# Loading the input beside the first mixer's prologue, and the last norm inside the MLP, in a four-layer decoder trunk

## What is computed

```python
def reference(x, ...):                     # x: (8, 2048, 1024) float32
    for i in range(4):
        h = rmsnorm(x, norm_mix[i])
        y = (mixer_a, mixer_b, mixer_c)[i % 3](h, ...)   # A in layers 0 and 3
        x = x + y
        h = rmsnorm(x, norm_mlp[i])
        x = x + jnp.square(jax.nn.relu(h @ m_w1[i])) @ m_w2[i]
    return rmsnorm(x, norm_final)

def rmsnorm(x, g):
    return x * lax.rsqrt(jnp.mean(x * x, axis=-1, keepdims=True) + EPS) * g

def mixer_a(h, w_in, b_in, vn_g, vn_b, w_s, b_s, w_out):
    u, v = jnp.split(jax.nn.gelu(h @ w_in + b_in), 2, axis=-1)   # 3072 each
    v = layernorm(v, vn_g, vn_b)
    w = jnp.where(causal, w_s, 0)          # 8 groups of 128 x 128
    gate = einsum over each chunk of 128 tokens of w and v, plus b_s
    return (u * gate) @ w_out
```

## Time and profile before

| | |
|---|---|
| runs shown | 4108.21 and 4675.72 us, median 4391.97 us |
| the profiled execution, its own time | 4105.52 us |
| its span on the slowest core (6) | 4104.0 us |
| spans of the eight cores | 4067.6 to 4104.0 us |
| mean granted TensorE clock, cores | 0.932 to 0.943 of 2.4 GHz |
| busy share of core 6 | TensorE 91%, DVE 55%, ACT 25%, POOL 6% |

### The profile page before, as it was taken

The page is one execution under the profiler, slowest core; times in us unless marked ns, Lnnn a source line. Parts: engine busy times, 40 slices in busy tenths (PEclk is TensorE's granted clock), DMA queues, the critical chain, the costliest instruction groups (busy, mean ns, idle before and its releaser), DMA issues.

```text
span 4104.0 us, 48667 instructions; the slowest of 8 cores (4067.6 to 4104.0 us)
## 1 busy us (share of the span) xinstructions
PE 3716.4 (91%) x16824; PEld 1640.3 (40%) x16824; DVE 2253.4 (55%) x2975; ACT 1037.3 (25%) x1543; POOL 242.5 (6%) x278
## 2 busy tenths in 40 slices
PE   5899998999976799998998969999789999899995
PEld 3334443444432244443333324444334444344443
DVE  3425524756566765655556566566354353565655
ACT  2433332211111121112223231111243333211113
POOL 0011111000000000000000000000001111000000
PEclk7899998999988799999999979999789999899997
DMA  7689989122226512223323322220769899612202
GB/s 151 94 119 127 144 119 128 21 42 42 35 44 91 77 21 42 42 32 59 46 40 49 48 38 42 37 36 1 108 90 130 111 137 131 90 32 42 35 8 82
DMA packets 302184, 283.38 MB, mean 69 GB/s; under 512 B 4854, under 2 KB 281462, under 8 KB 301944
## 3 DMA queue, kind: packets, MB, share of 16 engines
q0 software_dynamic: 295104, 262.16, 44.5%
q1 hardware_dynamic: 6844, 18.12, 1.3%
HBM read 534.02 MB, written 8.39 MB: 132 GB/s over the span
## 4 chain that ended last, share of the span: by engine, by line
PE 84%; DVE 9%; ACT 3%; issue 3%; DMA 1%; ACTq 0%; DVEq 0%; SPq 0%; POOL 0%; POOLq 0%
PE bank L83 84%; DVE rsd L83 2%; ACT rsq L83 2%; DVE m_hT L83 1%; DVE hTp L83 1%; DVE c_dg L83 1%; DMA xin<-x 1%; DVE f_h L83 1%; DVE b_tA L83 1%; ACT c_yb L83 0%; DVE c_rstd L83 0%; DVE b_pooled L83 0%; DVE b_tB L83 0%; ACT rsd L83 0%; DVE b_y L83 0%
## 5 line engine op out<-in xcount | busy, mean ns | idle before, releaser
L83 DVE TENSOR_TENSOR xT<-bank,xT 128x512 f32<-128x512 f32 x1152 | 794.3, 691 | 462.7 <-PE bank L83 458.2
L83 PE MATMUL bank<-m_aT,ring 128*128 128x512 bf16 x4096 | 910.2, 381 | 15.2 <-DVE m_rl L83 15.2
L83 PE MATMUL bank<-m_hT,ring 128*128 128x512 bf16 x4096 | 908.3, 380 | 0.0
L83 PE MATMUL bank<-hTp,ring 128*128 128x512 bf16 x2560 | 624.4, 398 | 70.5 <-DVE hTp L83 39.5
L83 ACT ACTIVATE m_aT<-m_rl 128x512 bf16<-128x512 f32 x512 | 321.8, 629 | 1420.3 <-DVE m_rl L83 1420.3
L83 DVE TENSOR_SCALAR m_rl<-bank 128x512 f32<-128x512 f32 x512 | 352.5, 691 | 518.8 <-PE bank L83 394.9
L83 PEld LDWEIGHTS bank<-m_aT,ring 128*128 128x128 bf16 x4096 | 401.8, 98 | 504.0 <-issue 25.0
L83 PEld LDWEIGHTS bank<-m_hT,ring 128*128 128x128 bf16 x4096 | 401.9, 98 | 486.1 <-issue 5.6
L83 PEld LDWEIGHTS bank<-hTp,ring 128*128 128x128 bf16 x2560 | 252.6, 102 | 360.3 <-issue 152.5
L83 PE MATMUL bank<-ring,hTp 128*128 128x512 bf16 x1536 | 369.3, 384 | 19.8 <-DVE hTp L83 19.8
L83 PE MATMUL bank<-a_uT,ring 128*128 128x512 bf16 x1536 | 347.8, 391 | 9.2 <-DVE a_uT L83 9.2
(11 more groups left out here) (89 smaller groups left out, 1813.5 us busy)
## 6 DMA issues: line engine op xcount, KB each, us to landing
ring<-a_w_in POOLq DMA_DIRECT2D x96, 1024.0 KB, 11.2
ring<-m_w POOLq DMA_DIRECT2D x64, 1024.0 KB, 9.2
ring<-a_w_out POOLq DMA_DIRECT2D x64, 768.0 KB, 7.7
ring<-c_w_in POOLq DMA_DIRECT2D x16, 1024.0 KB, 10.8
xin<-x SPq DMA_DIRECT2D x16, 512.0 KB, 5.7
ring<-b_w_in POOLq DMA_DIRECT2D x8, 1024.0 KB, 8.7
ring<-b_w_out POOLq DMA_DIRECT2D x8, 1024.0 KB, 9.3
ring<-c_w_out POOLq DMA_DIRECT2D x8, 1024.0 KB, 10.0
```

Source lines behind the costliest of these rows:

```text
L83: return lambda e: getattr(e, _method)(*args, **kwargs)
```

## The change

1. **Input and first prologue together.** In layer 0 `mixer_a` calls the input phase itself. The prologue is now a generator with three yields. Its first part (four loads, the memsets) is issued after x chunk 1, the part to the masked matrices after chunk 6, the column sums after chunk 10, a_S after chunk 13; the norm of tile 0 after chunk 3.
2. **The mask.** The affine select on POOL becomes a multiplication on DVE, straight from PSUM, by a mask tile that POOL makes once at the start.
3. **Layer 3.** The norm of tile 0 stands ahead of the whole prologue, which has the new mask too.
4. **The last norm.** The output phase is a function `tail(tt)`, called in the last layer's MLP right after W2 of fb 7 for that tile. It transposes the raw xT, takes the sum of squares on ACT from PSUM (one number per token), the root and reciprocal on 128 x 1, and scales on DVE from PSUM by that number and by a tile that holds the norm's weights in every partition, loaded once.

```diff
     for c in range(NCH):
         ...
+        if after_chunk is not None:
+            after_chunk(c)
...
+            def rn0():
+                rmsnorm(rb_persist, 0, gcol, lambda kc: hTp[0][:, kc, :], lambda kc: hTp_res[0][kc])
...
+                def prologue():
...
+                    sc.op("sp", I("dma_start", out=wst[:], in_=dram["a_w_s"][ia].rearrange("g t s -> t g s")),
+                          wr=[wst_res], dma=asem)
+                    sc.op("sp", I("dma_start", out=bsrc[:], in_=dram["a_b_in"][ia:ia + 1, AW:2 * AW]),
+                          wr=[bsrc_res], dma=asem_b)
+                    sc.op("dve", I("memset", sel1[:], 1.0), wr=[sel1_res])
+                    sc.op("dve", I("memset", rrow[:], 0.0), wr=[rrow_res])
+                    sc.op("dve", I("memset", lrow[:], 0.0), wr=[lrow_res])
+                    sc.op("dve", I("memset", lrow[32:33, :], 1.0), wr=[lrow_res])
+                    sc.op("sp", I("dma_start", out=rrow[32:33, :], in_=dram["a_b_s"][ia:ia + 1, :]), wr=[rrow_res], dma=asem_r)
+                    sc.op("sp", I("dma_start", out=lrow[0:1, :], in_=dram["a_vn_b"][ia:ia + 1, :]), wr=[lrow_res], dma=asem_l)
+                    yield
+                    sc.op("dve", I("tensor_copy", out=brow[:], in_=bsrc[:]), rd=[bsrc_res], wr=[brow_res])
...
-                sc.op("pool", I("affine_select", out=wmf2[:], in_=wmf[:], pattern=[[0, 8], [1, 128]],
-                                                        compare_op=ALU.is_ge, fill=0.0, base=0, channel_multiplier=-1),
-                      rd=[wmf_res], wr=[wmf2_res])
+                        sc.op("dve", I("tensor_tensor",
+                            out=wmf2[:, half * 4:half * 4 + 4, :], in0=bk[:].rearrange("p (a b) -> p a b", a=4),
+                            in1=cmask[:].unsqueeze(1).broadcast_to([128, 4, 128]), op=ALU.mult),
+                            rd=[bres, const_res], wr=[wmf2_res])
...
+                gen = prologue()
+                if with_input:
+                    def after_chunk(c):
+                        if c in (1, 6, 10, 13):
+                            next(gen, None)
+                        if c == 3:
+                            rn0()
+                    input_phase(pro, after_chunk)
...
+                else:
+                    rn0()
+                    for _ in gen:
+                        pass
...
-            RN(0)
             V(0)
...
+                if tail is not None and fb == 7:
+                    tail(tt)
...
+                if final:
+                    for half in range(2):
+                        bk, bres = bks[half]
+                        sc.op("act", I("activation", out=junk[half][:], in_=bk[:], func=AF.Square,
+                                       accum_out=ss[:, ob, half:half + 1]),
+                              rd=[bres], wr=[junk_res[half], ss_res[ob]])
+                    sc.op("dve", I("tensor_tensor", out=ss[:, ob, 2:3], in0=ss[:, ob, 0:1], in1=ss[:, ob, 1:2], op=ALU.add),
+                          wr=[ss_res[ob]])
+                    sc.op("act", I("activation", out=ss[:, ob, 3:4], in_=ss[:, ob, 2:3], func=AF.Sqrt,
+                                   bias=epst[:, 0:1], scale=1.0 / D), rd=[const_res], wr=[ss_res[ob]])
+                    sc.op("dve", I("reciprocal", out=ss[:, ob, 3:4], in_=ss[:, ob, 3:4]), wr=[ss_res[ob]])
+                    for half in range(2):
+                        bk, bres = bks[half]
+                        sc.op("dve", I("scalar_tensor_tensor", out=ost[ob][:, half * 512:(half + 1) * 512], in0=bk[:],
+                                       scalar=ss[:, ob, 3:4], in1=gbc[:, half * 512:(half + 1) * 512],
+                                       op0=ALU.mult, op1=ALU.mult),
+                              rd=[bres, ss_res[ob], gbc_res], wr=[ost_res[ob]])
```

More of the change, by code:

```diff
@@ L299, in evac_copy, with input_phase @@
             sc.op("dve", I("tensor_copy", out=out_ap, in_=in_ap), rd=rd, wr=wr)
-    with ExitStack() as ph:
+    def input_phase(stack, after_chunk=None):
         NXB = 4
-        xin = [sb(f"xin{i}", (128, D), F32, ph) for i in range(NXB)]
+        xin = [sb(f"xin{i}", (128, D), F32, stack) for i in range(NXB)]
         xin_res = [Res(f"xin{i}") for i in range(NXB)]
@@ L362, in add_to_x, with mlp @@
               rd=[bres], wr=[xT_res[dc][tt]])
-    def mlp(l):
+    def mlp(l, tail_setup=None):
         with ExitStack() as ph:
             rb = rb_persist
+            tail = tail_setup(ph) if tail_setup is not None else None
             hT = sb("m_hT", (128, KC, S), BF16, ph)
@@ L448, in mixer_a @@
[L448 to L457, removed]
@@ L464, in mixer_a @@
-                sc.op("sp", I("dma_start", out=lrow[0:1, :], in_=dram["a_vn_b"][ia:ia + 1, :]), wr=[lrow_res], dma=asem_l)
-                for half in range(2):
-                    bk, bres = next_bank()
-                    fns = [I("transpose",
-                        out=bk[:, j * 128:(j + 1) * 128], in_=wst[:, half * 4 + j, :], identity=ident[:]) for j in range(4)]
-                    sc.op("pe", fns, rd=[wst_res, const_res], wr=[bres])
-                    sc.op("dve", I("tensor_copy",
-                        out=wmf[:, half * 4:half * 4 + 4, :], in_=bk[:].rearrange("p (a b) -> p a b", a=4)),
-                        rd=[bres], wr=[wmf_res])
@@ L473, in mixer_a @@
-                sc.op("pool", I("affine_select", out=wmf2[:], in_=wmf[:], pattern=[[0, 8], [1, 128]],
-                                                        compare_op=ALU.is_ge, fill=0.0, base=0, channel_multiplier=-1),
-                      rd=[wmf_res], wr=[wmf2_res])
-                sc.op("act", I("activation", out=wmb[:], in_=wmf2[:], func=AF.Copy), rd=[wmf2_res], wr=[wmb_res])
-                for half in range(2):
-                    bk, bres = next_bank()
-                    sc.op("pe", I("matmul",
-                        bk[0:1, :], lhsT=onesf[:, 0:1], rhs=wmf2[:, half * 4:half * 4 + 4, :], start=True, stop=True),
-                        rd=[wmf2_res, const_res], wr=[bres])
-                    sc.op("dve", I("tensor_copy", out=rrow[0:1, half * 512:(half + 1) * 512], in_=bk[0:1, :]),
-                          rd=[bres], wr=[rrow_res])
@@ L916, in build_program @@
                 sc.op("sp", I("dma_start", out=out_d[c * 128:(c + 1) * 128, :], in_=ost[ob][:]),
                       rd=[ost_res[ob]], dma=osem[ob])
-        sc.wait_all("sp", osem)
-        sc.wait_all("sp", ["E_pe", "E_act", "E_dve"] + ring_sem)
+        return tail
+    first_is_a = bool(layers) and layers[0] % 3 == 0
+    if not first_is_a:
+        with ExitStack() as ph:
+            input_phase(ph)
+            sc.end_phase()
+    for li, l in enumerate(layers):
+        kind = l % 3
+        if kind == 0:
+            mixer_a(l, l // 3, with_input=(li == 0))
+        elif kind == 1:
+            mixer_b(l)
+        else:
+            mixer_c(l)
+        mlp(l, tail_setup=out_setup if li == len(layers) - 1 else None)
@@ L921, in build_program @@
+    if not layers:
+        with ExitStack() as ph:
+            tail = out_setup(ph)
+            for tt in range(NT):
+                tail(tt)
+    sc.wait_all("sp", osem)
+    sc.wait_all("sp", ["E_pe", "E_act", "E_dve"] + ring_sem)
     with nc.Block() as block:
```

126 lines of the change are left out of this document (71 added, 55 removed).

## The result

The changed kernel took 4046.96 us in the median (4032.76 to 4592.67, 11 runs), the kernel before 4191.92 us beside it (4105.44 to 4702.71, 10 runs). The ratio is 0.983, 95% interval 0.9813 to 0.9848: 1.7% less time. The profiled execution took 4032.8 us (span 4031.2, core 5) where that of before took 4105.5. That is 73 us less, where 64 were forecast (4041.5, range 4022 to 4066). The forecast was counted from the profiled execution of before, 4105.5, and not from the median of the runs shown, 4392.0, and is compared in the same way here. Its three terms do not all hold.

The account below looks back on a forecast made before the run. TensorE, busy 91% of the span, was taken as the bound, so gains come only where it waits. Head -17, layer 3's head -7 and tail -40 sum to -64: 4105.5 - 64 = 4041.5 us, range 4022 to 4066.

Parts of the forecast that it names:

- Head: Start until V(0) in layer 0: V(0) starts at 64.5 us instead of 81.82, -17 us, bounds -31 and -7.
- It costs less than it looks: Head, SP's queue: chunk 2 leaves at 19.6 us instead of 2.5, but weight loads use the engines meanwhile; x ends at 60.
- rule of turns: Head: each DMA engine alternates between queues with work, a packet at a time; x's end near 62, the whole at 4043 us.
- What is left of the 48 matmuls put behind chunk 13: Head, behind x's last chunk: its transposes and the remaining a_S matmuls take 2 to 7 us, taken as 4.5.
- the norm costs nothing: Head: tile 0's norm lies under coming chunks; eight banks absorb its 8.7 us on DVE; nothing charged, 2 us in the bound.
- Layer 3's head: From the last MLP matmul to V(0) in layer 3: 39.0 us instead of 46.1, -7 us, bounds -9 and -3.
- Tail: Behind the last MLP: last scaling ends at 4057.7 us against 4100.2, DVE pacing tail to tail; -40 us, bounds -48 and -25.
- A: Rival, tail: the clock falls in each tail, costing 2 to 3 us a tail, total 4049 us; chance 0.12.
- B: Rival, head: x starves behind weights and SP's new wait, x ends at 71, V(0) at 76, total 4052 us; chance 0.10.
- C: Rival, tail: a chunk's chain takes 3.5 us as hops through ACT cost more; tail -25, total 4056 us; chance 0.12.
- E: Rival, tail: square with a sum runs at the reciprocal's 3.35 us, slower than before, total 4116 us; chance 0.02.
- D: Rival, head and tail both better: x ends at 46, a chunk costs 2.2 us, total 4019.5 us; chance 0.12.

Follow-up runs that it names:

- e2_sp_late: Changed kernel with the two small DMAs into a_rrow and a_lrow issued behind x chunk 6, not chunk 1: 4010.83 us, ratio 0.9814 to the kernel before.
- e5_held: The kernel with both small DMAs behind chunk 6, plus the first five weight loads held until chunk 9 is copied: head 61.9 us, was 70.3.
- e4_k128: Changed kernel with a_lrow and a_rrow on 128 partitions instead of 33, added rows zero: 4009.96 us (one run) beside 4090.04 for the kernel before.
- e11_norm_late: The kernel with both small DMAs behind chunk 6, with tile 0's norm behind x chunk 12, not chunk 3: head 70.2 us, was 70.3.
- e1_tail_only: Kernel before with only the new tail; head and layer 3 as before: 4038.0 us beside 4090.0, ratio 0.9882.
- e9_pipe: Changed kernel with each tail chunk's two scalings issued behind the next chunk's one-column addition on VectorE: ratio 0.984 to the kernel before, last stage 485.6 us.
- e3_s_late: Changed kernel with the 48 a_S matmuls behind V(0) in both A layers, bias row by POOL's casting DMA: 4010.45 us, ratio 0.9809 to the kernel before.

## Why the prediction was right and wrong

**Head, -17 forecast, -7.9 measured: wrong.** The issue times were right. Two steps failed.
- "It costs less than it looks", of SP's new wait. The sum took x's end as 60 from work shares; x's last chunk landed at 67.2 in the median, past the 66 of "if the weights went first". With only four buffers x moves one chunk per landing, each landing is stretched by the other queue (8.5 us for 5.7), and the time lost at the start is not made up. Without the wait (e2_sp_late) the last chunk lands 7.6 us sooner and the head is 9.4 us shorter; with the weights held as well (e5_held) it is 8.4 us shorter again. The Trainium skill's rule of turns ("DMA: Bandwidth & Descriptors", section on queues, rings and completion order), by which the forecast estimated 62, had the right mechanism, and was 5 us short too: from 20 to 62 us both queues were served (60.9% and 46.3% of the engines).
- "What is left of the 48 matmuls put behind chunk 13 (8.53 us at half clock ...): 2 to 7 us, taken as 4.5". The block stands in TensorE's queue ahead of the transposes of chunks 14 and 15; all of it came behind chunk 13, and 12.0 us passed between x's end and V(0). It was read as an overlap with the wait for x, where an in-order queue makes it a delay of what x is needed for. Its price was misread too: the granted clock of the row of 8.53 us is 0.63 and not 0.50, and at 0.50 all along the block takes 10.6 us. With 128 rows it takes 6 (e4_k128).

That the norm costs nothing is not shown: without it behind chunk 3 x's end came 5.3 us sooner, and V(0) did not (e11_norm_late). The forecast left 2 us for it, in the bound.

**Layer 3's head, -7 forecast, -7.6 measured: right**, and term by term on core 5: norm 14.3 us (14.6 forecast), memsets 7.9 (7.84), cast 1.7 (1.75), masks 1.5 (1.5), sums 4.4 (4.8), a_S 8.8 (8.53).

**Tail, -40 forecast, -47.6 measured: right in mechanism, sizes off.** VectorE's queue did pace tail to tail. From the first group of transposes to the last scaling it took 67.4 us on core 5 and not 73.0. Terms: a chunk is 2.43 to 2.50 us in most places and not 2.6, and eight additions take 4.86 us and not 5.8 (three times 0.9), since back to back they come 0.61 apart where the mean of the earlier trace rows is of lone ones. The 2.5 us "given back for banks and clock" were hardly needed: the clock took 1.4 in the last tail. The measured -47.6 is at the better bound of -48; counted like the forecast, 2.2 us a chunk gives -46.4. e1_tail_only shows the whole term alone. TensorE was a bound close behind, as e9_pipe shows.

**The rivals.** A (clock falls in each tail) came true for the last tail alone, at 1.4 us; in each window from 3955 to 4015 the clock is 1.00. It was to follow from the Trainium skill's statement ("TensorE: Matmul & The Clock Gate", Part 4: PE-mode transpose) that transposes don't count for the clock. The tails test this only in part, as their transposes stand between blocks of matmuls. The fp32 transposes of the earlier trace rows do disagree: with nothing else on TensorE the clock there went from 0.50 (22 to 24 us) to 1.00 (26 to 28). B (x starves behind weights and SP's wait) came true in kind and nearly in size: it had x's end at 71, V(0) at 76 and -6, and 67.2, 77.7 and -6.4 by V(0)'s start were measured. C and E are out: the square with its sum takes 0.80 us, and no chunk took 3.5. D's tail came true, its head did not.

That the total came so near is luck: errors of +9 and -8 us met, and 7 us came that no step had.

## What to carry to other kernels

Work put into an in-order queue "while it waits" is free only if nothing behind it in that queue becomes ready first; count the whole block, at the clock it will get, as a delay of the item behind it. A load that has few buffers must not be queued behind a wait, even when the DMA engines are busy with something else; look for the consumer's true needs instead (V(0) needs 4 of 16 chunks; in the first layer that gave 21 us beyond e3_s_late, the 128 rows included). When a stretch is paced by one engine, shortening its work pays only until the next resource, here TensorE and its wait for a PSUM bank, or the start-up lag of a chain, which every cut of a block pays again.

## What the hardware did that was not expected

- For one block of 48 fp32 matmuls the granted clock depended on how many rows they use, and not only on TensorE being busy. With 33 rows: clock 0.50 with 2.00 of 2.00 us busy, 10.61 us; with 128 rows, most of them zero, 1.00 was reached within the block and it took 6.06 us. Begun at full clock, the 33-row block ran at 1.00 almost to its end once (5.65 us, e5_held, core 0) and fell to 0.50 within it another time (7.66 us, e3_s_late, core 1).
- On ScalarE a square with a sum out of PSUM (128 x 512) costs 0.60 us, and 0.20 us more for an instruction of its own that reads the sum out.
- VectorE's 512-column additions from PSUM come 0.61 us apart back to back where one alone shows 0.69.
